# A woven opening (x first, projection products between modulation units) and a rotary swap by transfers, in a four-layer diffusion transformer kernel on one core

## The reference, cut to what matters

```
for each layer:
    shift, scale, gate = split(silu(c) @ w_ada + b_ada, 3)        # for x; the same with c_ctx for ctx
    h = rms_norm(x, norm_g) * (1 + scale) + shift                 # 512 tokens x 2048
    p = h @ w_in                                                  # q, k, v, gates, ...
    q, k = rms_norm(q) , rms_norm(k)                              # per head of 128 (or 64) channels
    q, k = rope(q), rope(k)                                       # latent tokens only
    o = softmax(q k^T * scale) v                                  # latent: over ctx + latent
    x = x + gate * (concat(o_a * silu(g_a), o_b * silu(g_b)) @ w_out)

rope(x): x1, x2 = split(x, 2);  concat(x1 * cos - x2 * sin, x2 * cos + x1 * sin)
```

## Time and profile before

| | us |
|---|---|
| median of 3 runs | 3166.59 (3164.29 to 3167.61) |
| profiled execution | 3167.66 |
| its span | 3165.9 |
| TensorE busy | 3001.2 |
| VectorE busy | 1577.3 |
| ScalarE busy | 1025.7 |
| mean transfer rate | 156 GB/s |

### The profile page before, as it was taken

One profiled execution on the slowest core, in us unless ns is written; L12 is line 12 of the kernel. 1 busy time (PEld: TensorE's weight loads), 2 busy tenths in 40 slices (PEclk: granted clock), 3 DMA queues, 4 the chain that ended last, 5 costly groups with the idle time before them and its releaser, 6 DMA issues. The chain is left out here.

```text
span 3165.9 us, 41299 instructions
## 1 busy us (share of the span) xinstructions
PE 3001.2 (95%) x17364; PEld 2404.3 (76%) x17364; DVE 1577.3 (50%) x2497; ACT 1025.7 (32%) x1513; POOL 102.0 (3%) x157
## 2 busy tenths in 40 slices
PE   5899999999998999999889999999989989999988
PEld 4477777786776787887777779767767768897888
DVE  1334433355434554455555472655574355738574
ACT  2222233224312333333332221334442133225453
POOL 0000000000000000000000000430000000004000
PEclk6899999999998999999989999999999989999999
DMA  6844343321544553731755444324355433222455
GB/s 276 333 158 152 126 144 126 113 87 47 191 177 167 212 178 125 268 133 67 289 200 180 160 159 160 131 96 143 130 184 188 170 123 114 82 93 94 140 171 169
DMA packets 120136, 495.11 MB, mean 156 GB/s; under 512 B 11792, under 2 KB 30480, under 8 KB 95120
## 3 DMA queue, kind: packets, MB, share of 16 engines
q1 hardware_dynamic: 99648, 463.51, 41.2%
q10 hardware_dynamic: 20304, 28.97, 2.6%
HBM read 484.05 MB, written 8.39 MB: 156 GB/s over the span
## 5 line engine op out<-in xcount | busy, mean ns | idle before, releaser
L1359 PE MATMUL products<-h_high,w_high 128*128 128x512 f32 (+1 forms) x3424 | 1256.7, 367 | 77.7 <-DVE w_low L869 24.4
L1359 PE MATMUL products<-h_low,w_high 128*128 128x512 f32 (+1 forms) x3424 | 1191.9, 348 | 0.0
L1359 PE MATMUL products<-h_high,w_low 128*128 128x512 f32 (+1 forms) x3424 | 1191.4, 348 | 0.0
L869 DVE TENSOR_TENSOR w_low<-w_raw,w_high 128x1024 fp32r<-128x1024 f32 x500 | 614.3, 1230 | 804.5 <-ACT w_high L544 798.7
L544 ACT CAST w_high<-w_raw 128x1024 fp32r<-128x1024 f32 x500 | 524.6, 1049 | 1343.2 <-PE products L1359 1277.0
L1359 PEld LDWEIGHTS products<-h_high,w_high 128*128 128x128 f32 x3424 | 660.6, 193 | 272.0 <-issue 134.2
L1359 PEld LDWEIGHTS products<-h_low,w_high 128*128 128x128 f32 x3424 | 662.0, 193 | 83.6 <-issue 14.9
L1359 PEld LDWEIGHTS products<-h_high,w_low 128*128 128x128 f32 x3424 | 660.1, 193 | 80.9
L1359 PE MATMUL products<-w_high,h_high 128*128 128x256 f32 x640 | 184.2, 288 | 0.5 <-issue 0.5
L1359 PE MATMUL products<-w_high,h_low 128*128 128x256 f32 x640 | 181.0, 283 | 0.0
L1359 PE MATMUL products<-w_low,h_high 128*128 128x256 f32 x640 | 181.0, 283 | 0.0
(11 more groups left out here) (213 smaller groups left out, 2719.7 us busy)
## 6 DMA issues: line engine op xcount, KB each, us to landing
w_raw<-w_slots SPq DMA_DIRECT2D x500, 512.0 KB, 3.5
ada_w<-ada_slots SPq DMA_DIRECT2D x174, 1024.0 KB, 7.5
mix_b<-ada_slots SPq DMA_DIRECT2D x18, 1024.0 KB, 10.1
x_residual<-x ACTq DMA_DIRECT2D x2, 4096.0 KB, 23.0
x_scratch<-x_residual ACTq DMA_DIRECT2D x3, 2048.0 KB, 7.8
x_residual<-x_scratch ACTq DMA_DIRECT2D x3, 2048.0 KB, 9.1
x_residual<-ctx ACTq DMA_DIRECT2D x2, 2048.0 KB, 16.0
out<-x_residual ACTq DMA_DIRECT2D x1, 2048.0 KB, 7.8
```

The lines of the kernel that those rows point to most:

```text
L869: nc.vector.tensor_tensor(wlo[:, n % SPL, :], raw[:, n % RAW, :], whi[:, n % SPL, :].bitcast(F32), ALU.subtract).then_inc(low_done, 1)
L1359: ins = nc.tensor.matmul(o, a, b, start=first and q == 0, stop=last and q == 2, skip_group_check=skip)
```

## The change

It has two halves and a few small parts.

1. *Opening.* SP issues `cond`, `consts` and x before the units; ScalarE's queue issues select, bias and columns (the urgent ones) and then the tables that are needed later, on a semaphore of their own. The squares of x go to a ring of four buffers and VectorE adds them up; one set of token sums follows. The units' ring has six places (`Q`, `G` and `ada_w`). Blocks alternate between the PSUM banks `AD` and `B`. The first round's slots are ordered by quarter (`BY_QUARTER`: both groups for channels 0 to 511, then 512 to 1023, ...), and TensorE alternates one unit with one "part" (`opening_part`: one 128-channel chunk of one group, a quarter of a slot). The lambda computation moves behind the first chunks.
2. *Swap.* The permutation matmul is gone. SP copies the partition halves from the head buffer into `swapped` (in `pool_s`), 2 transfers of 64 partitions in layers 0 and 1 and 8 of 16 partitions in layers 2 and 3, and VectorE rotates one slot later for most groups. `swap` stands in SP's order behind the load of a slot.
3. *Broadcast.* ScalarE's copy of the broadcast root is gone in all layers; `scale_chunk` reads PSUM.

```diff
-ADA_RING = 4
+ADA_RING = 6
-OPEN_SLOTS = ((0, 1), (2, 3), (4,), (5, 6, 7))
+BY_QUARTER = tuple((j, s) for s in range(4) for j in range(2))
...
-        q_heads = {7: ("q", 0, 0), 8: ("q", 0, 1), 9: ("q", 1, 0), 10: ("q", 1, 1), 12: ("q", 2, 0), 13: ("q", 2, 1)}
+        q_heads = {7: ("q", 0, 0), 8: ("q", 1, 0), 9: ("q", 0, 1), 11: ("q", 1, 1), 12: ("q", 2, 0), 14: ("q", 2, 1)}
...
+        for ph in PH:
+            if ph["kind"] != "linear":
+                continue
+            for k, (kind, j, st) in ph["heads"].items():
+
+                if (kind, st) == ("k", 2) or (kind, st) == ("q", 0):
+                    e = HEAD_AT[(ph["layer"], kind, j)]
+                    SWAPS[ph["at"]["slot"] + k + (RAW if kind == "q" and j == 1 else RAW - 1)] = (ph["layer"], kind, j, e)
...
                 sp.dma_start(raw[:, n % RAW, :], ws[n, :, :]).then_inc(raw_landed[n % RAW], 16)
+                if n in SWAPS:
+                    swap(*SWAPS[n])
+
+            def swap(layer, kind, j, e):
+
+                sp.wait_ge(freed_dve, GROUP_FREED[e])
+                if kind == "k":
+                    sp.wait_ge(k_normed, KNORMS[e] + 1)
+                if e > 0:
+                    sp.wait_ge(roped, e)
+                buf = {"q": (Q, G), "k": (kb, k2)}[kind][layer // 2]
+                half = 64 if layer < 2 else 16
+                for p in range(0, P, half):
+                    sp.dma_start(swapped[p:p + half, :, :], buf[p ^ half:(p ^ half) + half, 2 * j:2 * j + 2, LAT]
+                                 ).then_inc(perm_done, 16)
...
                         if opens(ph, i):
+                            sp.dma_start(sc_in[:, :, :], dram["cond"]).then_inc(cond_in, 16)
+                            sp.dma_start(consts.ap(), dram["consts"]).then_inc(const_in, 16)
+                            sp.dma_start(xT[:, :, :], dram["x0"]).then_inc(x_in, 16)
                             for c in range(4):
-                                for u in range(8 * c, 8 * c + 8):
-                                    unit(u)
-                                for k in OPEN_SLOTS[c]:
-                                    slot(k)
+                                for half in range(2):
+                                    for u in range(8 * c + 4 * half, 8 * c + 4 * half + 4):
+                                        unit(u)
+                                    if c > 0:
+                                        slot(2 * c + half)
+                                if c == 0:
+                                    slot(0)
+                                    slot(1)
...
-                act.wait_ge(x_spread, layer + 1)
-                nc.scalar.copy(tmp[:, 2, :], SC[:, 1, :]).then_inc(x_ready, 1)
-
             def opening(evac):
 
-
+                act.wait_ge(ends["dve"], 1)
+                act.wait_ge(x_in, 16)
+                for t in range(KC):
+
+                    if t >= 5:
+                        act.wait_ge(x_added, t - 4)
+                    nc.scalar.activation(square_place(t), xT[:, t, :], ACT.Square).then_inc(sq_done, 1)
+                x_root(0)
+                act.wait_ge(const_in, N_CONST)
+                row_copy(0, 4)
+                high(0)
+                high(1)
+                row_copy(1, 8)
                 for c in range(4):
...
-                                                          tmp[:, 2, tk], ALU.mult, ALU.mult)
+                                                          SC[:, 1, tk], ALU.mult, ALU.mult)
...
+                for t in range(1, KC):
+
+                    dve.wait_ge(sq_done, t + 1)
+                    if t > 1:
+                        dve.wait_ge(x_added, t - 1)
+                    nc.vector.tensor_tensor(x_acc, x_acc, square_place(t), ALU.add).then_inc(x_added, 1)
+                x_root(0)
...
-                if s == (3 if kind == "k" else 1):
-
-                    dve.wait_ge(perm_done, e + 1)
+                if s == (3 if kind == "k" else 2 if j == 3 else 1):
+
+                    dve.wait_ge(perm_done, 16 * SWAP_DMAS[e + 1])
...
-                    rotate(x, B[:, :].rearrange("p (t n) -> p t n", t=2),
+                    rotate(x, swapped,
...
-                if s == (3 if kind == "k" else 0):
-                    if kind == "k":
-                        pe.wait_ge(k_normed, KNORMS[e] + 1)
-
-                    if e > 0:
-                        pe.wait_ge(roped, e)
-                    pe.wait_ge(freed_dve, GROUP_FREED[e])
-                    nc.tensor.matmul(B[:, :], PERM_HEADS[layer // 2], buf[:, 2 * j:2 * j + 2, LAT],
-                                     start=True, stop=True).then_inc(perm_done, 1)
...
+                    def opening_part(h):
+
+                        k, kk = h // KS, h % KS
+                        j, s = BY_QUARTER[k]
+                        if kk == 0:
+                            if s == 0:
+                                free_half(j)
+                            pe.wait_ge(low_done, k + 1)
+                        c = KS * s + kk
+                        if j == 0:
+                            pe.wait_ge(part_low, c + 1)
+                        ins = feature_chunk(k, j, kk, KS, hh[:, c, toks], hl[:, c, toks], w, c == 0, c == KC - 1)
+                        if kk == KS - 1:
+                            ins.then_inc(slot_used, 1)
+
+                    def opening():
+
+                        for u in range(8):
                             ada_unit(u)
...
+                            if u == 3:
+                                pe.wait_ge(x_added, KC - 1)
+                                token_sums(x_acc, 0, True).then_inc(x_sums, 1)
+                            if u == 4:
+                                ada_cols(0)
+                            if u == 5:
+                                x_broadcast(0)
+                        ada_cols(1)
+
+                        for c in range(1, 4):
+                            for k in range(8):
+                                ada_unit(8 * c + k)
+                                if k >= 2:
+                                    opening_part(8 * (c - 1) + k - 2)
+                                if k == 4:
+                                    ada_cols(2 * c)
+                            opening_part(8 * (c - 1) + 6)
+                            ada_cols(2 * c + 1)
+                            opening_part(8 * (c - 1) + 7)
+                        for h in range(24, 32):
+                            opening_part(h)
+                            if h == 31:
+                                head_side(ph, 7)
+                        for u in range(4 * ADA_FIRST, OPEN_UNITS):
+                            span_unit(u)
```

More of the change, by code:

```diff
@@ L113, in plan_phases @@
     add("opening")
-    at["ms"] += KC
     at["step"] += KC
@@ L359, in build @@
                         KROOTS_DONE[ph["layer"]] = KNORMS[-1]
+        for ph in PH:
[5 more added lines that the diff above has]
+                    SWAPS[ph["at"]["slot"] + k + (RAW if kind == "q" and j == 1 else RAW - 1)] = (ph["layer"], kind, j, e)
+        for e, layer in enumerate(sorted(v[0] for v in SWAPS.values())):
+            SWAP_DMAS.append(SWAP_DMAS[-1] + (2 if layer < 2 else 8))
         PARTS, n_parts = [], 0
@@ L712, in sub_side @@
                 nc.scalar.activation(tmp[:, 2, 0:w], G[:, t, toks], ACT.Square).then_inc(sub_sq, 1)
[L715 to L721 removed]
+            act.dma_start(sel.ap(), dram["select"]).then_inc(const_in, 16)
+            act.dma_start(adaB.ap(), dram["ada_bias"]).then_inc(const_in, 16)
+            act.dma_start(cols.ap(), dram["cols"]).then_inc(const_in, 16)
+            for place_in, name in ((lamv, "lambdas"), (ropeA.ap(), "rope_gqa"), (ropeB.ap(), "rope_mla"),
+                                   (pool_edge.ap(), "pool_edge")):
+                act.dma_start(place_in, dram[name]).then_inc(table_in, 16)
             for pi, ph in enumerate(PH):
@@ L972, in low_chunk, with lambda_sums, lambdas @@
                 last.then_inc(part_low, 1)
-            def opening(evac):
+            def lambda_sums():
+                dve.wait_ge(table_in, N_TABLES)
+                step(nc.vector.tensor_tensor(lamv[:, :, 0, :], lamv[:, :, 0, :], lamv[:, :, 1, :], ALU.mult))
+                own()
+                nc.vector.reduce_sum(lam[:, 0:4], lamv[:, :, 0, :], AX.X).then_inc(lam_sum, 1)
+            def lambdas():
+                dve.wait_ge(lam_exp, 1)
+                for l in range(2):
+                    step(nc.vector.scalar_tensor_tensor(
+                        lam[:, l:l + 1], lam[:, 4 + 2 * l + 1:6 + 2 * l], -lam_init(l),
+                        lam[:, 4 + 2 * l:5 + 2 * l], ALU.add, ALU.subtract))
+                    c = COL["subln"] + l
+                    step(nc.vector.tensor_scalar(cols[:, c:c + 1], cols[:, c:c + 1], 1.0 - lam_init(l), None,
+                                                 ALU.mult))
+            def opening(evac):
+                for t in range(1, KC):
[4 more added lines that the diff above has]
+                x_root(0)
```

(41 more changed lines are left out.)

117 lines of the change are left out of this document (44 added, 73 removed).

## The result

The changed kernel takes 3132.65 us (median of 4 runs, 3129.61 to 3136.16) beside 3167.1 us for the kernel before: ratio 0.9885, 95% interval 0.9872 to 0.9897. Forecast was 3106, in a range of 3088 to 3140. So it is 34.5 us faster where 61 were forecast, and some 26 us are to be explained. The profiled execution took 3129.61 us with a span of 3127.8.

A forecast was written before the change was run, and what follows sets the result against it. TensorE, busy 3001.2 of 3165.9 us, was taken to bound the kernel except in the opening, with its transfer holes. Opening −44, swaps −14.3 and roots −2 sum to −60.3, so 3106 us median; range 3088 to 3140.

The forecast's parts named there:

- low clock in the weave: Rival, opening: the clock stays low between units and products, a pass costs 39 us, total 3157 us; chance 0.08.
- transfers alone speed up nothing: Rival, opening: column, scale, chunk paces the weave; TensorE waits 3.6 us at three quarters, +11, 3117 us; no separate chance.
- The opening's size: Opening: slot 8 starts at 131 us against 175.9, counted as −44 us, with bounds −50 and −25.
- VectorE works 4 chunks × 4 × 0.48 = 7.7 us for the chunks and two casts of 1.2, which lies beside it: Opening, each pass: VectorE's work lies beside TensorE's 20.7 us and the transfers' 22.2 us, which bound the pass.
- The swaps: All layers: removing 26 swap matmuls gives −26.8 us, stalls cost +12.5, net −14.3; bounds −22 and +20.
- Layer 2, keys: Layer 2 key stages: two more units between them (1.9 us) leave 0.3 us of stall each, +1 us.
- the slow rival: Rival, SP's queue: swaps queued behind units take 13.7 us, +74, so 3180 us, slower than before; chance 0.03.
- Layer 3: Layer 3 stalls: keys 1.5 us four times, +6 us; queries +1.7 and +2.3, +4 us.
- The swap of eight: Layers 2 and 3: 4.0 us issue plus 2.3 landing, 6.3 us from its last wait; bounds 5.5 and 9.7.
- eight transfers are dear: Rival, swaps of eight 32 KB transfers: 3.6 us more per swap, near 3142 us, or 3140 from the rows; chance 0.14.
- Each further us of swap latency costs about 10 us: Swaps: ten places without slack, so each extra microsecond per swap adds about 10 us to the result.
- Roots: Broadcast root: VectorE no longer waits for ScalarE's copy, about 0.7 us with hand-over, three times in later layers; −2 us.

## Why the prediction was right, and where its sizes were off

**What bounds the kernel, and the opening's mechanism: right.** The hole in the transfers closed to 418 to 421 GB/s from 10 us on, and the clock stayed high in the weave, so the rival "low clock in the weave" is out. The rival "transfers alone speed up nothing" came true in the size that it named: TensorE waited 10.9 us for low parts at the three quarters, for 11 forecast. The additions came as forecast (0.69 us each, paced at 0.8 by their waits), and unit 7 with its columns ended at 42.3 us (forecast 42).

**The opening's size: −44 forecast, −30.4 in the trace** (slot 8 at 144.5, forecast 131). By the medians it is −31.0 (swaps by TensorE everywhere, less the kernel before without the root copy) to −33.8 (the changed kernel less the one with the old opening). The step that was mis-sized is "VectorE works 4 chunks × 4 × 0.48 = 7.7 us for the chunks and two casts of 1.2, which lies beside it". The work does lie beside, but one cast stands in the chain from columns to chunks and waits for a slot. Moving it behind the chunks gave 9.9 us, so it was the cast's place and not the chain of column, scale and chunk alone. The other 3.6 us (134.6 against 131) are put down to two things, the pace: from 58.2 to 60.8 and 63.4 us a unit and a half chunk take 2.58 us together, where I had 0.95 + 1.37 = 2.32, and to a clock of 0.89 between 110 and 126 us in the kernel with the moved casts. How the 3.6 divide, and whether that is all of it, was not tested.

**The swaps: −14.3 forecast; +1 to +3 measured, no gain that the intervals can show** (+3.3 between the two kernels with the old opening, +0.6 between those with the new one). For this half the direction was wrong as well as the size. The matmuls' −26.8 is borne out by the 10.4 us that ten swaps gave in the medians. The stalls were forecast at 12.5; the medians put them at 26.8 + 0.6 = 27 to 26.8 + 3.3 = 30. By term:
- Layer 2, keys: "Layer 2 has two units more between key stages (1.9 us), so 0.3 each: +1". This step failed. It took the units as TensorE's time to spare (and even so 1.5 − 1.9 leaves nothing, so its 0.3 has no working) and forgot them as bytes in the queue. The stall was 13.1 us, and 2.3 once the units stood behind the weight, so their place cost 10.8. With it falls the sentence that spoke against the slow rival, "every swap stands ahead of the units of its step, and units are loaded long ahead": it is the next weight that wasn't far enough ahead. Late weight loads in layer 2 were among the prediction's own signs of being wrong.
- Layer 3: forecast 6 + 4 = 10, found 12.1.
- Layer 1: forecast 1.5, found 1.0 and 4.3 in the two profiles of the changed kernel, and 1.6 to 4.2 by the same estimate in the eight other kernels whose swaps SyncE issues there.
- The swap of eight: forecast 4.0 + 2.3 = 6.3 us; measured from the normalized keys to the rotation 6.5 to 7.8 in layer 3 and 6.5 to 7.6 in layer 2, where the issue takes 5.04 to 6.12 and the landing 2.0 (median). The issue was the term to raise. The upper bound of 9.7 us, on which the rival "eight transfers are dear" rests, was not reached. VectorE in layer 3:

```profile
2653.56 1.23 DVE L1087 TENSOR_TENSOR k_diff<-k_diff,tmp 128x1024 f32<-128x1024 f32 x1
...
2661.32 0.69 DVE L1112 TENSOR_TENSOR tmp<-pool_sums,rope_heads 128x512 f32<-128x512 f32 x1 [5.41 <-DMA pool_sums<-k_diff]
```

- "Each further us of swap latency costs about 10 us": 11.8 measured. The forecast counted waits alone; the measured figure holds the lower clock behind them too (0.92 in slots 260 to 280), so the nearness of the two is in part luck.

**Roots: −2 forecast, −3.4 measured**; the difference is inside the interval.

**The sum.** Opening −31.0, root −3.4 and swaps +0.6, or −33.8, −3.4 and +3.3: both make −34, the difference measured beside these runs, as they must, since they are differences of the same medians. Of the 26 us short of forecast, the opening has 10 to 13 and the swaps 15 to 18; the root gives 1 back. The total lay inside the range of 3088 to 3140 because its upper part was laid out for dear transfers; two terms missed in the same direction, and the second half gained nothing, so that the number fell inside is in part luck. The stalls in the windows of layers 2 and 3 are 25.2 us, and with the 4.3 of layer 1 in the same profile 29.5, which is all that the medians ask for. What stays open: why GpSimd's queue paused in a swap, and what makes layer 1 differ from profile to profile.

## What to carry to other kernels

A transfer that replaces a short matmul is paid for in its queue: count the issue time of every piece, then look at what is queued next and by when the engine behind it needs it; units or other bulk loads belong behind the weight that is due first. In a woven order, nothing that waits for a free buffer may stand between a result and the small operations that hand it on. And two profiles of one program tell how much of a difference between two programs means nothing: here 10 us of span, some 8 of them the clock.

## What the runs showed of the hardware

- The granted clock in stretches with 3.3, 2.6 and 5.9 us of idle time differed between two executions of one program (1.00 or 0.92, 1.00 or 0.94, 1.00 or 0.98), worth 6.5 us in the three.
- TensorE's queue of one-column matmuls was busy for 20.66 of 22 us at a granted clock of 0.50; with 512-column products between the units it was busy for 20.83 of 22 us in the same window at 0.92.
- A small transfer inside the core's memory takes SyncE's queue about 0.63 us from start to start (5.04 us for eight) and GpSimd's 0.50 (3.97 for eight), and from SyncE it lands in 1.8 us at 16 KB, 2.0 at 32 KB and 2.6 to 3.3 at 128 KB (medians). The Trainium skill ("DMA: Bandwidth & Descriptors", "Issuing engine by pattern") calls the queues of SyncE and ScalarE generally faster; for the landing the trace agrees (2.0 against 2.1 to 2.2 us), for the issue it has the reverse.
